# A two-block transformer kernel on one core: the second block's mixer in a new instruction order, with packed recurrence levels and negated scores

## The reference

```python
z = h @ w_in                                # 256 x 3352
(hq, hf, hi, hgt, nq_, kc_, vc_, ks_, vs_, kw_, vw_, ng_) = jnp.split(z, offsets, axis=-1)
o_hg = hgrn2(hq, hf, hi, hgt, lbs[l], hg_norm_g[l])     # gated linear recurrence, 4 heads of 128
o_nsa = nsa(...)          # 8 heads of 64: compressed, selected and windowed attention, gated
mix = jnp.concatenate([o_hg, o_nsa], axis=-1) @ w_out[l]
x = x + gt1 * mix
# in hgrn2, per chunk: A[t, s] = sum_k q[t] * exp(b[t] - b[s]) * k[s] for s <= t, b = cumsum(log f)
#                      o = A @ v  (+ the state carried in)
# attention: p = exp(scores - max) / sum
```

## Time and profile before

| | us |
|---|---|
| median of 3 runs (1346.29 to 1348.22) | 1347.31 |
| the profiled execution's own time | 1346.13 |
| its span, first to last instruction | 1344.3 |

### The profile page before, as it was taken

The page is one execution under the profiler, slowest core; times in us unless marked ns, Lnnn a source line. Parts: engine busy times, 40 slices in busy tenths (PEclk is TensorE's granted clock), DMA queues, the critical chain, the costliest instruction groups (busy, mean ns, idle before and its releaser), DMA issues.

```text
span 1344.3 us, 22621 instructions
## 1 busy us (share of the span) xinstructions
PE 1314.2 (98%) x8928; PEld 1198.0 (89%) x8928; DVE 1054.9 (78%) x1814; ACT 698.9 (52%) x1124; POOL 54.4 (4%) x104
## 2 busy tenths in 40 slices
PE   7999999999999999999999999999999998999998
PEld 6999999998888889999999988888879876888887
DVE  4688668886778785877687777788899887698888
ACT  5554544444454455555534364454458566655554
POOL 1111000000000000000000000000010000000000
PEclk9999999999999999999999999999999998999999
DMA  8865445663767654444446655778625503345551
GB/s 282 245 212 187 172 157 196 214 230 135 274 254 283 258 192 171 159 163 154 155 168 215 229 197 216 272 272 295 235 94 193 199 32 129 132 180 198 190 190 63
DMA packets 42787, 262.00 MB, mean 195 GB/s; under 512 B 5613, under 2 KB 6381, under 8 KB 15422
## 3 DMA queue, kind: packets, MB, share of 16 engines
q1 hardware_dynamic: 32688, 227.28, 46.5%
q0 software_dynamic: 9904, 33.24, 7.8%
q10 hardware_dynamic: 94, 0.07, 0.0%
HBM read 258.99 MB, written 1.58 MB: 194 GB/s over the span
## 4 chain that ended last, share of the span: by engine, by line
PE 90%; DVE 6%; ACT 2%; issue 1%; DMA 0%; SPq 0%; DVEq 0%; ACTq 0%
PE psum L738 23%; PE psum L758 16%; PE psum L855 12%; PE psum L744 12%; PE psum L764 9%; PE psum L803 4%; PE psum L829 2%; PE psum L810 2%; DVE split L1828 1%; PE psum L833 1%; PE psum L916 1%; PE psum L894 1%; PE psum L906 1%; PE psum L1025 1%; PE psum L703 1%
## 5 line engine op out<-in xcount | busy, mean ns | idle before, releaser
L1828 DVE TENSOR_TENSOR split<-ring,split 128x1024 fp32r<-128x1024 f32 x406 | 480.1, 1221 | 68.9 <-ACT split L1337 67.6
L1337 ACT CAST split<-ring 128x1024 fp32r<-128x1024 f32 x405 | 405.7, 1049 | 168.7 <-PE psum L744 82.1
L738 PE MATMUL psum<-h,split 128*128 128x256 f32 x2176 | 273.2, 283 | 0.2 <-ACT split L1337 0.2
L738 PEld LDWEIGHTS psum<-h,split 128*128 128x128 f32 x2176 | 265.8, 192 | 1.6 <-issue 0.8
L758 PE MATMUL psum<-h,split 128*128 128x512 f32 x960 | 228.9, 390 | 0.0
L758 PEld LDWEIGHTS psum<-h,split 128*128 128x128 f32 x960 | 177.8, 188 | 35.3
L855 PE MATMUL psum<-split,feed 128*128 128x512 f32 x792 | 185.5, 390 | 0.1
L855 PEld LDWEIGHTS psum<-split,feed 128*128 128x128 f32 x792 | 146.7, 188 | 29.8 <-DVE split L1828 0.5
L744 PE MATMUL psum<-h,split 128*128 128x256 f32 x1088 | 142.0, 283 | 0.2 <-DVE split L1828 0.2
L744 PEld LDWEIGHTS psum<-h,split 128*128 128x128 f32 x1088 | 135.6, 192 | 0.4 <-DVE split L1828 0.4
L764 PEld LDWEIGHTS psum<-h,split 128*128 128x128 f32 x960 | 123.3, 191 | 4.8
(11 more groups left out here) (328 smaller groups left out, 1402.9 us busy)
## 6 DMA issues: line engine op xcount, KB each, us to landing
ring<-stream SPq DMA_DIRECT2D x213, 1024.0 KB, 4.8
arena<-ada POOLq DMA_DIRECT2D x48, 512.0 KB, 5.3
arena<-bias_by_distance POOLq DMA_DIRECT2D x32, 96.0 KB, 4.8
gain<-norm_rows POOLq DMA_DIRECT2D x4, 512.0 KB, 7.1
x<-x_in SPq DMA_DIRECT2D x2, 512.0 KB, 4.4
ring<-stream SPq DMA_DIRECT2D x2, 512.0 KB, 6.9
gain<-mod_rows POOLq DMA_DIRECT2D x2, 512.0 KB, 3.9
out<-x SPq DMA_DIRECT2D x4, 256.0 KB, 2.0
```

The lines of the kernel that those rows point to most:

```text
L738: pe.matmul(to[m], w[0][:, at + k, cols[m]], rhs[:, part, at + k, :], start=m == parts[0] and k + part == 0, stop=False)
L1337: act.copy(split_of(x)[:, 0, n], ring[:, AT[x] % RING, n]).then_inc(wh_ready, 1)
L1828: return dve.tensor_tensor(out_, value, high.bitcast(F32), ALU.subtract)
```

## The change

The computed result is the same. Nine edits:

1. **Order.** The mixer's steps stand in a new order on PE, ACT and DVE. The pieces of `hi`, `hg` and `out` (a chunk and one tile of tokens, 12 matmuls) are cut in two (`ks=(0, 1)` and `ks=(2, 3)`), and other steps stand between the quarters.
2. **Packed levels.** Levels 1 to 7 multiply only the queries of the late half of each block: 64 columns for a head and tile, not 128. A level then fills one bank, banks 6 and 7 alternate, and `level(i)` waits for `level_read_(i-2)`. The masked copy of such a level has 512 elements, not 1024.
3. **Negated scores** (both blocks): the scores are multiplied by minus the scale, DVE takes a minimum, ACT's exponential has scale -1. The instruction that negated the maximum is gone, 12 times in the mixer, 32 times in the first block.
4. **Key factor.** Four multiplications of `hk` by a per-channel factor leave DVE; the factor is applied to `hq` in ACT's copy, now two of 256 elements instead of one of 512.
5. **`gathered`**: 8 operations of 240 elements, not 16 of 120.
6. **`rope`**, twice: 5 operations for 10.
7. **`scaled_queries`, `scaled_keys`**: 1 and 3 operations for 2 and 6.
8. **`query_sums`, `key_sums`**: 1 operation for 2, each.
9. The table of cosines: 2 operations for 4.

The core of the diff (the orders cut; three places of them stand below):

```diff
-                    pe.wait_ge(level_read, i)
+                    pe.wait_ge(level_read, max(1, i - 1))
+                else:
+                    pe.wait_ge(qk_ready, NT + 1)
                 last = i == HG_STEPS - 1
                 for hd in range(HG):
                     for m in range(1 if last else 2):
-                        q_, k_ = (hq, hk) if i == 0 else (hqh, hkh)
-                        mm = pe.matmul(bank[6 + hd // 2][:, (hd % 2 * 2 + m) * P:(hd % 2 * 2 + m + 1) * P],
-                                       k_[:, hd, m * P:(m + 1) * P],
-                                       q_[:, hd, (1 if last else m) * P:(2 if last else m + 1) * P],
-                                       start=True, stop=True)
+                        tile = slice(m * P, (m + 1) * P)
+                        if i == 0:
+                            to, k_, q_ = bank[6 + hd // 2][:, (hd % 2 * 2 + m) * P:(hd % 2 * 2 + m + 1) * P], hk, hq[:, hd, tile]
+                        else:
+                            late = slice(hd * P, (hd + 1) * P) if last else slice((2 * hd + m) * P // 2, (2 * hd + m + 1) * P // 2)
+                            to, k_, q_ = bank[6 + i % 2][:, late], hkh, hq_late[:, i % 2, late]
+                        mm = pe.matmul(to, k_[:, hd, tile], q_, start=True, stop=True)
...
             def level_read_(i):
                 dve.wait_ge(level_done, i + 1)
-                if i < HG_STEPS - 1:
+                if 1 <= i < HG_STEPS - 1:
+                    dve.wait_ge(level_read, i)
...
+                elif i < HG_STEPS - 1:
+                    w, at = LEVELS[i - 1], P + (i - 1) * P // 2
+                    mask = pair_mask[:, at:at + P // 2].rearrange("p (c t) -> p c t", t=w)
+                    ins = dve.copy_predicated(
+                        A_in.rearrange("p h m (c b t) -> p (h m) c b t", b=2, t=w)[:, :, :, 1, :],
+                        mask.unsqueeze(1).broadcast_to([P, 2 * HG, P // (2 * w), w]),
+                        bank[6 + i % 2].rearrange("p (x c t) -> p x c t", x=2 * HG, t=w))
...
             def queries_(i):
                 dve.wait_ge(hexp_q, i)
-                if i >= 2:
-                    dve.wait_ge(level_done, i)
-                else:
-                    dve.wait_ge(qh_ready, 1)
-                dve.tensor_tensor(blocks_of(hqh, i)[:, :, 1, :], blocks_of(hq, i)[:, :, 1, :],
+                dve.wait_ge(qh_ready, 1)
+                if i >= 3:
+                    dve.wait_ge(level_done, i - 1)
+                dve.tensor_tensor(hq_late[:, i % 2, :].rearrange("p (x t) -> p x t", t=2 ** (i - 1)), blocks_of(hq, i)[:, :, 1, :],
                                   blocks_of(hE, i)[:, :, 1, :], ALU.mult).then_inc(qh_ready, 1)
...
-                    ins = dve.tensor_tensor_reduce(S2[u % 2][:, at], bank[u % 2][:, at], mask, HD ** -0.5, NEG,
-                                                   ALU.add, ALU.max, stat(u, 0, groups)[:, g:g + 1])
+                    ins = dve.tensor_tensor_reduce(S2[u % 2][:, at], bank[u % 2][:, at], mask, -HD ** -0.5, -NEG,
+                                                   ALU.add, ALU.min, stat(u, 1, groups)[:, g:g + 1])
                 ins.then_inc(s2_read, 1)
-                dve.wait_ge(s2_read, u + 1)
-                dve.tensor_scalar(stat(u, 1, groups), stat(u, 0, groups), -1.0, None, ALU.mult).then_inc(negmax2, 1)
...
-            rows("hg", 0, h, 0, (4, 5), parts=(0,))
-            turn2(1)
-            rows("hg", 0, h, 0, (4, 5), parts=(1,))
+            rows("hg", 0, h, 0, (4, 5), parts=(0,), ks=(0, 1))
+            rows("hg", 0, h, 0, (4, 5), parts=(0,), ks=(2, 3))
+            rows("hg", 0, h, 0, (4, 5), parts=(1,), ks=(0, 1))
```

More of the change, by code:

```diff
@@ L1248, in _ @@
             values2(1)
-            scores2(3)
-            turn2(4)
-            level(7)
+            level(8)
             turn2(5)
+            hg_output()
             values2(2)
-            level(8)
+            turn2(6)
             scores2(4)
-            hg_output()
-            turn2(6)
             turn2(7)
+            values2(3)
+            turn_hg()
             scores2(5)
-            values2(3)
             turn2(8)
-            pe.wait_ge(hg_read, 1)
-            turn_hg()
+            rows("out", 0, feed, 0, (4, 5), parts=(0,), ks=(0, 1))
@@ new lines, in values_out, with second_out @@
+            def values_out():
+                job_wait("vv", 0)
+                act.copy(vn, halves(5)).then_inc(act_evac, 1)
+            def second_out():
+                act.wait_ge(zeroed, 7)
+                act.wait_ge(w2_done, 1)
+                for g in range(2):
+                    half, at = slice(g * HD, (g + 1) * HD), slice(g * NCMP, (g + 1) * NCMP)
+                    act.copy(kcmp[half, at], bank[2][half, at])
+                for i in range(4):
+                    rows_ = slice(32 * i, 32 * i + 32)
+                    e = act.copy(V4[rows_, i], bank[2][rows_, HD:3 * HD].rearrange("p (g d) -> p g d", g=2))
+                e.then_inc(w2_copied, 1)
@@ L1726, in _ @@
-            act.copy(PcT, bank[2].rearrange("p (g t) -> p g t", g=2)).then_inc(cmp_copied, 1)
-            exps2(3)
-            split_high((L, "out", 0), halves_=(1,))
+            compressed_turned()
+            split_high((L, "out", 0), (0,))
+            query_exp(8)
             copy_turned2(2)
@@ L2573, in _ @@
-            keys_(7)
             softmax2_in(6)
-            key_exponent(8)
             hg_gates()
-            level_read_(7)
-            queries_(8)
-            keys_(8)
+            level_read_(8)
             softmax2_in(7)
-            level_read_(8)
             softmax2_out(6)
+            hg_gains()
             softmax2_out(7)
+            hg_sums()
+            low_mix(0)
             softmax2_in(8)
-            hg_sums()
+            hg_scaled()
+            hg_mixed()
             softmax2_in(9)
-            low_mix(0)
+            softmax2_out(8)
@@ L2588, in _ @@
+            hg_low()
             split_low((L, "out", 0), 1)
[L2589 to L2592 removed]
             softmax2_out(9)
```

576 lines of the change are left out of this document (315 added, 261 removed).

## The result

| | before | after |
|---|---|---|
| median, us (4 runs each) | 1347.76 (1346.29 to 1348.83) | 1335.40 (1334.29 to 1335.90) |
| the profiled execution's own time | 1346.13 | 1335.90 |
| its span | 1344.3 | 1334.1 |

The ratio after to before is 0.9908, 95% interval 0.9891 to 0.9925: faster by 12.4 us. By the interval the gain lies between 10 and 15 us. Two further sets of runs of the changed kernel on other chips gave 0.9907 (0.9894 to 0.9920) and 0.9906 (0.9891 to 0.9921), with medians of 1335.73 and 1334.50. The mean granted clock of a whole execution was 0.997 to 1.000 in all 13 executions of the changed kernel and 0.992 to 0.996 in the 36 executions of the kernel before that ran beside the experiments.

A forecast was written before the change was run, and what follows sets the result against it. PE's waits and slow clock were taken as the bound, 15.0 us; less 3.0 tail waits, 1.8 clock fall and 0.7 middle leaves 9.5, so 1336.6, plus 1.2 to the median: 1337.8 us, range 1332.5 to 1343.

The forecast's parts named there:

- What bounds the kernel: Second block's mixer, up to `out` 2: PE loses 8.6 us idle and 6.4 us to slow clock, 15.0 together.
- Packed levels on PE: The recurrence's 7 levels: 64 moving columns cost PE what 128 do, so nothing gained; other bound 6.2 us.
- columns count: Rival: the 7 packed levels save PE time too, 6.2 us, giving 1331.6; chance 9%.
- DVE's terms: Mixer work on DVE falls from 111.2 to about 102 us; masked copies save 4.4, `gathered` takes 3.5.
- Quarters fill the waits: Mixer on PE: 12 matmuls cut into 6 and 6, placed behind nearly every level and `turn2`; no separate size.
- First block's negations: First block on DVE: 32 operations, at most 11 us, hidden under PE, so removing them gains nothing.
- The new tail: PE around and behind `hg_output`: waits of 0.3, 1.8, 0.7 and 0.2 remain, 3.0 us together.
- One clock fall: Mixer's tail: PE's clock falls once behind two nearby waits, costing 1.8 us; bounds 0 and 3.6.
- The middle: Between the recurrence's levels: PE waits for DVE at close places such as `level(3)`, 0.7 us; bounds 0 and 7.
- New waits in the middle: Rival: DVE, as full as before, delays 7 levels by 3.5 to 7 us, giving 1341.3 to 1344.8; chance 22%.
- Given back behind the mixer: Rival: late feed-forward chunks cost up to 4.8 us each; two late give 1347.4, no change; chance 6%.
- The recurrence's loop decides: Rival: the cross-engine chain makes 8 levels late, 1.5 us each adds 12 us, giving 1349.8; chance 5%.

The follow-up runs named there:

- run 5: Changed kernel with the masked copy of each packed level issued twice on DVE; 1339.46 us, ratio 0.9939 to the kernel before.
- run 4: Changed kernel with each pair of quarter pieces joined at the place of the first one; 1339.59 us, ratio 0.9948 to the kernel before.
- run 1: Changed kernel with the old order on PE, ACT and DVE and uncut pieces, all other edits kept; 1343.39 us, ratio 0.9983 to the kernel before.
- run 3: Changed kernel with new order and packed levels, but the small steps of before (negations, key factor, unmerged operations) in both blocks; 1337.44 us, ratio 0.9928.
- run 8: Changed kernel with a tiny square root on ACT behind the squares, so the root's table load comes early; 1336.14 us, ratio 0.9920.
- run 7: Changed kernel with `copy_turned2(7)` put ahead of the recurrence's root on ACT; 1337.41 us, ratio 0.9931 to the kernel before.
- run 6: Changed kernel with two idle copies of 1024 elements on ACT behind the root, lengthening the wait at `values2(3)`; 1337.64 us, ratio 0.9931.
- run 2: Changed kernel with old order, uncut pieces and unpacked levels, only negated scores, key factor and merged small steps kept; 1344.44 us, ratio 0.9982.

## Why the prediction was right, and where it was off

**What bounds the kernel (15.0 us in waits and slow clock): right.** Of the 8.6 us of idle time 5.3 went, of the 6.4 us of clock loss all. PE's busy time fell by 6.45 with the same matmuls, some 6 of it by the clock, so the loss worked out from the granted clock was real time.

**Packed levels on PE, nothing: right.** 1.72 us for 16 records of 64 columns, 1.79 for 16 of 128. The rival *columns count* falls: its 6.2 us are not there, and the sentence of the Trainium skill (page "TensorE: Matmul & The Clock Gate", section "What happens when you issue a matmul") that throughput is N cycles does not hold for these short fp32 matmuls, each of which has a weight load of its own.

**DVE's terms: two too large.** DVE's work in the mixer fell by 7.1 us, from 113.4 to 106.3, and I had it fall by some 9. The packed copies saved 10.5 - 6.2 - 1.3 = 3.0, not 4.4: I gave all seven 0.69, and the two of the shortest runs took 1.30, the price of the unpacked copy. I had named this case as a bound and not given it to those two. `gathered` takes 4.2 us (8 operations of 0.56), not 3.5. DVE was busy for 86.5% of the new stretch, not 84%. Neither moved the time visibly, but run 5 says that the load is near its limit: 5.8 us more of it cost 3.6.

**Quarters fill the waits: right,** and worth 3.4 us (run 4). **The order** is worth the rest, 4.1 us: without it and the quarters 7.5 of 11.5 us are missing, with the same DVE work (run 1), and 3.4 of these are the quarters. **First block's negations, nothing:** the stretch starts no earlier than before (1009.8 against 1008.6), and run 3, which has them again, starts at 1011.4. Part of this spread is the clock: only in the profiles of the kernel before and of run 8 was it 1.00 all the way to the stretch, and these two start at 1008.60 and 1008.29. So the term is some 0.3 us, by one profile each.

**The new tail, 3.0 us of waits: right.** 0.3, 1.6, 0.9 and 0.3 against my 0.3, 1.8, 0.7 and 0.2. Which engine and which instruction end each wait is as worked out. Run 7 confirms the chain from the other side: whichever of the two ACT serves first, the other's customer waits.

**One clock fall, 1.8 us: this step was off; it measured 0.** I took 1.8 and 0.7 us of wait so near each other as one of 2.5 and compared it with the 2.42 of before. The clock stayed at 1.00, in all three profiles of the changed kernel. The price of a fall was about right: 1.3, 1.3, 1.5 and 1.65 us in runs 8, 7, 6 and 5. What was wrong is that it came, and the runs show how near it was: run 8 has the same sum of waits with 1.77 as the last one, and the clock fell. It fell behind 0.75 (run 5), 0.68 and then 1.77 (run 8), 2.99 (run 7), 3.48 (run 6) and 2.19 (run 2), and did not behind 1.60 and then 0.91, nor behind 2.23 in run 1. So the length of the wait alone does not order the cases.

Nor does the kernel. My forecast leaned on the wait of 1.79 at 983.93, behind which the clock stayed whole. The same place in two profiles of the changed kernel, the first one and the second one, each with the start of what follows:

```profile
984.86 2.10 PE L805 MATMUL psum<-nq_beside,h 128*128 128x512 f32 x8 [1.79 <-DVE h L1915]
986.80 1.09 PE L812 MATMUL psum<-nq_beside,h 128*128 128x512 f32 x4
...
984.26 2.83 PE L805 MATMUL psum<-nq_beside,h 128*128 128x512 f32 x8 [1.78 <-DVE h L1915]
986.88 1.91 PE L812 MATMUL psum<-nq_beside,h 128*128 128x512 f32 x4
```

The program is the same and the wait is the same to 0.01 us, and the same eight matmuls took 1.94 us in the first and 2.62 in the second. The granted clock from 984 to 992 us was 1.00 in the first and 0.79 in the second; in the third profile, behind 1.78, it was 0.79 too. So the length of a wait can't tell whether this fall comes, and one row in which it stays away is weak evidence that it will stay away again. What decides stays open. For the tail this means that the changed kernel's missing fall is seen three times and each fall of runs 5 to 8 once; their medians lie 3.7, 1.9, 1.7 and 1.6 us above the changed kernel's beside them, which agrees with their stretches.

**The middle, 0.7 us: also 0.** No level waited, the second bank let PE go on. With these two terms at what they measured, and the waits at 3.2, the sum is 15.0 - 3.2 = 11.8 us for the stretch, against 11.7 by the same windows.

**From the sum to the median.** The two profiled executions differ by 10.2 us and not by 11.6, since the changed kernel's stretch began 1.2 us later and what stands behind it took 0.2 longer. The medians differ by 12.4 because the profiled execution of before lay 1.6 us below the median of these runs, and that of after 0.5 above. My 1.2 us from one execution to the median went the wrong way. So of the 2.4 us between the forecast of 1337.8 and 1335.4, the two terms that measured 0 make 2.5; that the rest cancels to so little is luck.

**The chances.** Most of the 9%, a third of the 22% and the last two cases (11%) are about a quarter, not the "about 2 in 10" that I gave for a time outside the range.

**Rivals.** *New waits in the middle*: none. *Given back behind the mixer*: 204.6 against 204.4 us, no. *The recurrence's loop decides*: no level is late.

## What to carry to other kernels

Where PE is near full, read each wait together with the granted clock behind it: here a wait of 0.75 us cost 2.4, and a change that took 5.3 us of waits away got some 6 us of slow clock back as well. Do not plan on a fall, or on its absence, from one profile: look at the same place in several. Cut the large groups of matmuls in pieces and put these where a wait would be; that was worth 3.4 us and took no work from any engine. When two customers hang on one engine's queue, work out the chain of both before their order is changed: both attempts to serve one of them earlier (runs 7 and 8) made the last wait longer and brought the slow clock back.

## What the runs showed of the hardware that was not expected

- A masked copy of 512 elements per partition took 1.30 and 1.31 us at levels 1 and 2, where it writes runs of 1 and 2 elements, and 0.70 to 0.74 at the five others, with runs of 4 to 64. One of 1024 elements took 1.32. The price goes with the length of the run, up to a factor of 1.8.
- TensorE's granted clock fell to half behind a wait of 0.75 us at one place, and stayed whole behind one of 2.23 at another. At one and the same place, behind 1.78 and 1.79 us in the same program, it fell in two of three profiles. The falls of runs 5 to 8 cost 1.3 to 1.65 us each.
- In the old order the kernel with packed levels has the same waits as the one without and a stretch 1.8 us shorter, most of it through one clock fall less. Whether packing or chance took that fall away is not shown.
- Halving the columns of a matmul from 128 to 64 took 0.42 us from seven levels of 16 matmuls each, where half of their 12.66 us would be 6.3.
